# The up blocks of the wide feed-forward chunks as three 256-column products, without a copy and a sum of halves

## What is computed

```python
SEQ, D, FF = 256, 1024, 2816

def _swiglu(x, wg, wu, wd):
    return (jax.nn.silu(x @ wg) * (x @ wu)) @ wd

# second block, twice per layer; the first block has the same form once
h = _swiglu(_rmsnorm(x, g[0]), ffn_w_gate[l, 0], ffn_w_up[l, 0], ffn_w_down[l, 0])
x = x + 0.5 * _rmsnorm(h, g[1])
```

## Time and profile before

| | us |
|---|---|
| median of 3 timed executions | 1300.43 |
| lowest and highest | 1299.01, 1300.94 |
| the profiled execution | 1302.19 |
| its span, first to last instruction | 1300.5 |
| TensorE with a matmul under way | 1281.0 |
| TensorE with a weight load under way | 1076.5 |
| VectorE busy | 867.0 |
| ScalarE busy | 731.5 |
| mean granted TensorE clock, share of full | 0.997 |

### The profile page before, as it was taken

How to read it: one execution, slowest core, us unless ns; L and a number is a source line. 1 busy time by engine, 2 the same in 40 slices (tenths; PEclk the granted TensorE clock), 3 DMA queues, 4 the chain that set the end, 5 groups by cost and what they waited for, 6 DMA issues and landing times.

```text
span 1300.5 us, 19942 instructions
## 1 busy us (share of the span) xinstructions
PE 1281.0 (99%) x7343; PEld 1076.5 (83%) x7343; DVE 867.0 (67%) x1157; ACT 731.5 (56%) x1102; POOL 126.0 (10%) x120
## 2 busy tenths in 40 slices
PE   8999999999999999999999999999999999999998
PEld 6887788888888888877888888888887897888886
DVE  4476687554876666676766666766666687766665
ACT  4343554445655555757655556655557656755553
POOL 3000099000550000010000000000000100000000
PEclk9999999999999999999999999999999999999999
DMA  9996386556465555562555564655663543455561
GB/s 337 360 401 219 127 282 231 185 186 201 140 216 194 182 185 199 191 184 75 194 187 190 189 202 144 203 186 191 194 224 116 175 143 121 165 192 192 194 210 65
DMA packets 177125, 252.62 MB, mean 194 GB/s; under 512 B 9336, under 2 KB 143796, under 8 KB 177076
## 3 DMA queue, kind: packets, MB, share of 16 engines
q1 hardware_dynamic: 174080, 243.28, 56.7%
q0 software_dynamic: 2624, 8.48, 1.7%
q10 hardware_dynamic: 372, 0.19, 0.1%
HBM read 248.73 MB, written 1.05 MB: 192 GB/s over the span
## 4 chain that ended last, share of the span: by engine, by line
PE 89%; DVE 4%; ACT 3%; SPq 1%; DMA 1%; issue 1%; DVEq 0%; ACTq 0%
PE ps L745 25%; PE ps L638 14%; PE ps L639 13%; PE ps L640 13%; PE ps L742 13%; PE ps L678 1%; PE ps L686 1%; PE ps L679 1%; PE ps L1085 1%; PE ps L662 1%; DMA raw<-in_conv_w_in 1%; DVE w_lo L1785 1%; DVE w_lo L1780 1%; PE ps L948 1%; SPq L517 1%
## 5 line engine op out<-in xcount | busy, mean ns | idle before, releaser
L745 PE MATMUL ps<-xT_pair,w_hi 128*128 128x512 f32 x1440 | 393.0, 394 | 0.0
L1780 DVE TENSOR_TENSOR w_lo<-raw,w_hi 128x2048 fp32r<-128x2048 f32 x111 | 260.9, 2352 | 99.8 <-ACT w_hi L1271 99.6
L745 PEld LDWEIGHTS ps<-xT_pair,w_hi 128*128 128x128 f32 x1440 | 246.1, 189 | 33.0
L1276 ACT ACTIVATE w_hi<-raw,par 128x512 fp32r<-128x512 f32 x336 | 215.4, 715 | 102.2 <-PE ps L745 101.4
L1271 ACT ACTIVATE w_hi<-raw 128x2048 fp32r<-128x2048 f32 x111 | 211.6, 1908 | 74.4 <-PE ps L640 41.9
L742 PEld LDWEIGHTS ps<-xT_pair,w_lo 128*128 128x128 f32 x1440 | 220.4, 189 | 30.3 <-DVE w_lo L1785 0.4
L1785 DVE SCALAR_TENSOR_TENSOR w_lo<-raw,par,w_hi 128x512 fp32r<-128x512 f32 x336 | 231.6, 752 | 12.8 <-ACT w_hi L1276 12.7
L742 PE MATMUL ps<-xT_pair,w_lo 128*128 128x256 f32 x1440 | 229.3, 281 | 0.1
L638 PE MATMUL ps<-w_lo,hT_hi 128*128 128x512 f32 x400 | 156.9, 392 | 0.0
L639 PE MATMUL ps<-w_hi,hT_hi 128*128 128x512 f32 x400 | 156.2, 390 | 0.0
L640 PE MATMUL ps<-w_hi,hT_lo 128*128 128x512 f32 x400 | 155.7, 389 | 0.0
(11 more groups left out here) (290 smaller groups left out, 1630.1 us busy)
## 6 DMA issues: line engine op xcount, KB each, us to landing
raw<-in_ffn_w_gate SPq DMA_DIRECT2D x88, 512.0 KB, 4.0
raw<-in_ffn_w_up SPq DMA_DIRECT2D x88, 512.0 KB, 4.9
raw<-in_ffn_w_down SPq DMA_DIRECT2D x88, 512.0 KB, 4.2
raw<-in_ffn_w_in SPq DMA_DIRECT2D x44, 512.0 KB, 4.7
raw<-in_conv_w_in SPq DMA_DIRECT2D x24, 512.0 KB, 9.7
raw<-in_fox_w_in SPq DMA_DIRECT2D x24, 512.0 KB, 4.5
raw<-in_ffn_w_out SPq DMA_DIRECT2D x22, 512.0 KB, 4.2
raw<-in_ab_w_in SPq DMA_DIRECT2D x14, 512.0 KB, 4.5
```

What stands on the lines that cost most here:

```text
L745: mm = pe.matmul(ps[:, bank, :].rearrange("p (s c) -> p s c", s=2), hi[:, cols[k]], xT_pair[:, :, 4 * u + k, :], start=False, stop=u == 1 ...
L1276: a = act.activation(w_hi[:, slot_of(n), c], raw[:, slot_of(n), c], ACT.Copy, scale=par[:, g + k:g + k + 1])
L1780: dve.tensor_tensor(w_lo[:, slot_of(n), :], raw[:, slot_of(n), :], w_hi[:, slot_of(n), :].bitcast(F32), ALU.subtract).then_inc(raw_done, 1)
```

## The change

The up blocks (2 and 3) leave wide_part for a new function, narrow_part. It makes each block of three products of 256 columns for each of the four input slices: w_lo by xT_hi, w_hi by xT_hi, w_hi by xT_lo, all accumulated into columns 0 to 255 of the bank. So the sum of the three is complete in PSUM. up_rest, its ScalarE copy and the VectorE sum go, with the semaphores up_rest_ok and up_sum. VectorE multiplies the PSUM columns by silu at once, and waits for w_used where ScalarE did. TensorE waits for hid_wide in place of up_sum. Gate blocks stay as they are.

```diff
+            def narrow_part(n, u, blocks, j=0):
+                hi, lo = unit(n, j)
+                for b in blocks:
+                    o = ps[:, WIDE_BANK[b], 0:SEQ]
+                    cols = [slice(k * 512 + b * P, k * 512 + (b + 1) * P) for k in range(4)]
+                    for k in range(4):
+                        pe.matmul(o, lo[:, cols[k]], xT_hi[:, 4 * u + k, :], start=u == 0 and k == 0, stop=False, skip_group_check=True)
+                        pe.matmul(o, hi[:, cols[k]], xT_hi[:, 4 * u + k, :], start=False, stop=False, skip_group_check=True)
+                        mm = pe.matmul(o, hi[:, cols[k]], xT_lo[:, 4 * u + k, :], start=False, stop=u == 1 and k == 3, skip_group_check=True)
+                return mm
...
-                    wide_part(n, 1, (2, 3), j).then_inc(w_used, 1)
+                    narrow_part(n, 1, (2, 3), j).then_inc(w_used, 1)
...
-                wide_part(n - 1, 0, (2, 3), 1).then_inc(w_used, 1)
+                narrow_part(n - 1, 0, (2, 3), 1).then_inc(w_used, 1)
...
-                    pe.wait_ge(up_sum, v - 1 + i)
-                    wide_part(n - 1, 0, (2, 3), i).then_inc(w_used, 1)
+                    pe.wait_ge(hid_wide, v - 1 + i)
+                    narrow_part(n - 1, 0, (2, 3), i).then_inc(w_used, 1)
...
-                pe.wait_ge(up_sum, v + WIDE)
+                pe.wait_ge(hid_wide, v + WIDE)
...
-                    act.wait_ge(w_used, v + 3 * j)
-                    act.activation(up_rest, ps[:, 0:2, SEQ:2 * SEQ], ACT.Copy).then_inc(up_rest_ok, 1)
...
-                    dve.wait_ge(up_rest_ok, WIDE * f + j)
-                    dve.tensor_tensor(hid, ps[:, 0:2, 0:SEQ], up_rest, ALU.add).then_inc(up_sum, 1)
-                    dve.wait_ge(up_sum, WIDE * f + j)
+                    dve.wait_ge(w_used, weight_count(n) + 3 * j)
                     dve.wait_ge(sil_wide, WIDE * f + j)
-                    dve.tensor_tensor(hid, hid, sil, ALU.mult).then_inc(hid_wide, 1)
+                    dve.tensor_tensor(hid, ps[:, 0:2, 0:SEQ], sil, ALU.mult).then_inc(hid_wide, 1)
```

More of the change, by code:

```diff
@@ L349, in block_program @@
         sil_wide = sem("sil_wide")
-        up_rest_ok = sem("up_rest_ok")
-        up_sum = sem("up_sum")
         hid_wide = sem("hid_wide")
```

## The result

The changed kernel takes 1308.27 us (median of 11, 1305.28 to 1309.84) against 1300.94 (11 runs, 1299.01 to 1304.4) for the kernel before. The two medians lie 7.3 us apart; the ratio of the executions is 1.0048, with a 95% interval of 1.0038 to 1.0057, which is 6.2 us slower. Forecast were 1307.2 us and a ratio of 1.0052. Two slow executions further down, one of e1 (5011.1 us at a mean granted clock of 0.243 of full) and one of e6 (1704.97 us at 0.691), are in no ratio and no median here.

The account below looks back on a forecast made before the run. TensorE's rate of starting matmuls was taken to bound the kernel. 180 up blocks at +0.0375 us gave +6.75, removed work counted as nothing, so 1300.43 + 6.75 = 1307.2 us, range 1302.8 to 1310.0.

Parts of the forecast that it names:

- What bounds the kernel: Wide chunks: TensorE's rate of starting matmuls sets the end; a chunk of 16.69 us is a solid run of matmuls.
- stated high end: Whole kernel: top of the forecast range, 1310.0 us; a narrow start of 0.1215 us would give +10.0 us.
- The term 180 x 0.0375 us: Up blocks of the wide chunks: 180 blocks, each 0.0375 us dearer, add 6.75 us.
- one block price: Wide chunks: a block costs 1.4025 us now, four starts at 0.118 and four at 0.2325; a narrow one 1.440.
- Removed work at nothing: ScalarE copy and VectorE sum, 27 and 31 us busy, stand beside the down product; dropping them gains nothing.
- cover of the moved wait: TensorE before the next chunk's up blocks: the multiply ends early enough, slack 4.7 us, so the later wait costs nothing.
- Rival 1: Narrow up blocks: 256-column starts stay 0.118 us apart, 1.416 us a block, +2.5 us, 1302.9 us; chance 8%.
- Rival 2: Narrow up blocks: fixed cost per matmul near nothing, 0.1175 us a start, +1.4 us, 1301.8 us; chance 3%.
- Rival 3: Narrow up blocks: repeated hi weights load free, 0.114 us a start, -6.2 us, 1294.2 us; chance 3%.
- Rival 4: Entry of 90 narrow runs or the loop's back edge: 0.10 us dearer each, +9 us on top, 1316 us; chance 4%.
- Rival 5: VectorE multiply: the w_used wait makes it late, so the change does not do what it says; chance 1%.
- What would show it: Profile after: 8063 matmuls, 1.44 us a block, 16.84 a chunk, VectorE 31 and ScalarE 27 us less busy, span not following.

Follow-up runs that it names:

- e1: Changed kernel with wide up blocks again, copy and sum left out, so w_hi by xT_lo is missing from the up product; 1300.47 us, ratio 0.9998 to before.
- e6: Kernel before with the token tile laid out so that a wide matmul's 512 columns are contiguous; 1300.64 us, ratio 1.0002.
- e2: Kernel before with narrow_part for the up blocks, ScalarE's copy and a second VectorE operation kept in place; 1307.3 us, ratio 1.0053.
- e10: Kernel before with wide chunks reordered so that all 256-column matmuls of a chunk form one run; 1294.93 us, ratio 0.996.
- e3: e2 with the gate blocks also made by narrow_part, copies and second VectorE operations kept; 1313.91 us, ratio 1.0103 to the kernel before.
- e9: Kernel before with w_lo by xT_hi left out of the up blocks; 1214.94 us, one profiled execution, no ratio.
- e11: Kernel before with two blocks' low parts, then two blocks' wide parts together, runs of 8 and 8; 1297.32 us, ratio 0.998.
- e12: Changed kernel with its matmuls reordered into two runs of 256 columns a chunk; 1304.54 us, ratio 1.0027 to the kernel before.
- e8: Kernel before with 256- and 512-column matmuls in turn in all wide blocks, in place of four and four; 1305.11 us, ratio 1.004.
- e4: Changed kernel with each up block's twelve matmuls grouped by product, four of each; 1306.83 us, ratio 1.0049 to the kernel before.
- e7: Changed kernel with the token tile laid out so that a wide matmul's 512 columns are contiguous; 1306.77 us, ratio 1.0041 to before.

## Why the prediction was right, point by point

**What bounds the kernel: right.** e1 and e2 separate the halves; only the matmuls count. 45 chunks by 0.149 us are 6.7 us, and the ratio says 6.2 (4.9 to 7.4). (The stated high end, 1310.0, is 0.4 below its own sum, 1300.43 + 10.0; the 1308.27 measured lies under both.)

**The term 180 x 0.0375 us: right in size, for a reason half understood.** The narrow start at 0.1200 held in every run and every order. But 0.2325 us is no property of a wide start, nor 0.118 of a low one. Three numbers give most of the periods: 0.1200 us for a start of 256, 0.2267 for one of 512 (e10's down product), and 0.019 us for each change from 256 to 512 and back. The last one is fitted from e10 and the kernel before, (16.685 - 16.554)/7, so these two are no test of the sum; the others are.

| kernel | starts of 256, 512 | changes | sum us | measured |
|---|---|---|---|---|
| before | 32, 56 | 8 | 16.69 | 16.685 |
| changed | 64, 40 | 5 | 16.84 | 16.834 |
| e3 | 96, 24 | 1 | 16.98 | 16.980 |
| e9 | 16, 56 | 4 | 14.69 | 14.720 |
| e10 | 32, 56 | 1 | 16.55 | 16.554 |
| e11 | 32, 56 | 4 | 16.61 | 16.614 |
| e12 | 64, 40 | 2 | 16.79 | 16.786 |

So the change costs 16 x (2 x 0.1200 - 0.2267) = 0.213 us a chunk for replacing 16 wide starts by 32 narrow ones, and gets back 3 x 0.019 = 0.057, since five runs of 256 columns are left of eight. The net is 0.156, measured 0.149. The prediction had both in one block price, because it took 1.4025 us from blocks that contained their change of width. That this came out to 1 ns a chunk (0.150 against 0.149) is partly luck of the order: the four blocks replaced had held four changes, and replacing them took away three. e12 shows it: with changes already rare, the same narrow blocks cost 10.4 us.

Two runs are outside the sum. In e8, 32 changes with one start between cost 16.791 - 16.535 = 0.256 us, 8 ns each. e9 takes 0.03 us a chunk more than its sum. So 19 ns is an average over the orders tried and no constant of one change. Behind 8 wide starts (e11) or 16 (e10) it is over: the down product's first five starts take 1.13 us there (1179.23 to 1180.36) and 1.14 (1176.92 to 1178.06). Where only four stand behind the low parts, it reaches into the wide starts that follow, as e9's up blocks and the down product of the kernel before show; in the changed kernel's chain above, the down product's first five starts take 1.16 us as well (200.99 to 202.15), there behind 24 narrow ones. Why it goes on was not tested.

**Removed work at nothing, cover of the moved wait: right.** e1 ran as before within 0.1%, and the slack grew from 4.7 to 7 us.

**Rival 1 (discount survives at 0.118): wrong**, 1.440 us a block, and e4 shows no 0.118 in groups of low parts either; the discount belongs to the first starts behind wide ones. **Rival 2 (a fixed cost near nothing): wrong** here. The Trainium skill (TensorE: Matmul & The Clock Gate, section Back-to-back issue gap) gives N/2.4 + 2.5 ns for isolated matmuls; the starts measured here carry 13.3 ns on top of 256/2.4 = 106.7, and 13.4 on top of 512/2.4 = 213.3. **Rival 3 (repeated weights free): wrong**, see e4. **Rival 4 (dearer entries): not there** for the narrow run's first start; what I didn't see is that an entry does cost, and on the other side: the wide starts behind a narrow run pay some 25 ns together, not 100, and they paid as much behind the low parts before. **Rival 5: no**.

**What would show it.** The signs came as named but for two. ScalarE is 23.3 us less busy and not 27. The span moved by 4.8 and not 6.7 us: 1 us is the opening stage, and the seams between layers are shorter by the rest. What the seams gain from was not examined. Nor do the runs say where in TensorE the cost of a change of width arises.

## What to carry to other kernels

Where TensorE starts matmuls without a gap, its time is above all a count of starts by width: here 0.120 us for 256 columns and 0.227 for 512, so two products fused into one wide start win 13 ns, and the copy and sum that fusing needs cost nothing here, where the other engines had slack. Take spacings from starts, never from durations (281 and 394 ns here), and check whether they depend on the neighbours, before a spacing is used as a price. Then order the matmuls so that those of one width stand together: that alone brought 0.4% here, with no work removed.

## What the runs showed of the hardware

- The 512-column starts behind a run of 256-column ones together cost 23 to 26 ns more than further on (rows rounded to 10 ns), for a run of 8 in e11, 24 in the changed kernel and 32 in e10. Where four such starts are followed by other 512-column ones, these cost some 20 to 30 ns more too (eight in e9, five in the kernel before). The first starts of 256 behind 512 are some 10 ns cheaper together. The periods give 19 ns net for each change, 8 where widths alternate start by start (e8), and 26 in e9, (14.720 - 14.615)/4.
- Reading 512 columns as two pieces 8 KB apart costs the same as reading them in one (e6, e7).
- A start of 128 columns costs 0.111 us, hardly less than one of 256 (0.120). That the weight load is the limit there is the likeliest reading, and was not tested apart.
- The opening stage of unchanged code varied by 3 us from one execution to another, and the granted clock goes with it: part of the stretches 28 to 36 and 145 to 151 us runs at 1.2 GHz in some executions and not in others (0.72 against 1.00 in the second), though the code of that stage is the same. The mean clock and the time of whole executions go together too: of the kernel before, beside e1, 1298.74 us at 1.0 and 1303.93 at 0.996.
